# Two side chains of a two-layer trunk on one Trainium2 core: a compact block inverse, a respaced attention, and a shorter weight ring

## The reference

```python
h = x
h = h + gated_deltanet(rms_norm(h), ...)       # layer 0: 32 value heads of 128, 16 key heads
h = h + swiglu_ffn(rms_norm(h), ...)           # hidden width 5632
shared_kv = nsa_shared_kv(h, ...)              # six 512-wide projections, two of them compressed
h = h + nsa_attention(rms_norm(h), shared_kv)  # layer 1: 16 heads, 4 groups of K/V
h = h + swiglu_ffn(rms_norm(h), ...)
return rms_norm(h, final_norm_g)
...
# DeltaNet, per head and chunk: (I + strictly lower(beta k k^T decay)) is inverted, then
v_new = u_c - w_c @ state
o_c = q_c @ state + attn_qk @ v_new
state = state * exp(gl) + k_c^T @ v_new
# attention, per query block: three branches, each a softmax, summed with sigmoid gates
return gb[0] * o_cmp + gb[1] * o_slc + gb[2] * o_win
```

## Time and profile before

| | us |
|---|---|
| three runs, median (lowest to highest) | 2998.84 (2996.97 to 2998.98) |
| the profiled execution, its own time | 3000.31 |
| its span, first to last instruction | 2998.5 |
| TensorE busy in it | 2896.9 |
| VectorE busy | 1837.0 |
| ScalarE busy | 1328.9 |
| mean granted TensorE clock | 0.982 of full |
| read from HBM | 490.02 MB |

### The profile page before, as it was taken

The page is one execution under the profiler, slowest core; times in us unless marked ns, Lnnn a source line. Parts: engine busy times, 40 slices in busy tenths (PEclk is TensorE's granted clock), DMA queues, the critical chain, the costliest instruction groups (busy, mean ns, idle before and its releaser), DMA issues.

```text
span 2998.5 us, 37768 instructions
## 1 busy us (share of the span) xinstructions
PE 2896.9 (97%) x14080; PEld 2433.9 (81%) x14080; DVE 1837.0 (61%) x2200; ACT 1328.9 (44%) x1539; POOL 26.4 (1%) x29
## 2 busy tenths in 40 slices
PE   7999999999999999999999999889989999999997
PEld 6888888888887788888888878778778888888886
DVE  5777877877777645555555554556655555555555
ACT  6445454453543444444444444544435444444443
POOL 0000000000000000000000000000000000000000
PEclk9999999999999999999999999899999999999999
DMA  6333443434433345555555545532325555555553
GB/s 268 136 131 121 165 150 125 161 131 144 159 114 112 140 183 194 185 194 192 188 194 182 195 176 185 197 113 96 129 85 199 194 191 187 191 189 194 188 190 112
DMA packets 69411, 493.11 MB, mean 164 GB/s; under 512 B 7712, under 2 KB 8032, under 8 KB 10592
## 3 DMA queue, kind: packets, MB, share of 16 engines
q1 hardware_dynamic: 68112, 487.95, 45.4%
q10 hardware_dynamic: 1232, 4.23, 0.4%
HBM read 490.02 MB, written 2.13 MB: 164 GB/s over the span
## 4 chain that ended last, share of the span: by engine, by line
issue 57%; PE 40%; DVE 1%; ACT 1%; POOL 0%; DMA 0%; POOLq 0%; ACTq 0%; SPq 0%; DVEq 0%
PE ACC L483 12%; PE ACC L485 12%; PE ACC L484 12%; PE SIDE L491 2%; PE SIDE L772 1%; PE SIDE L751 0%; PE ACC L714 0%; PE SIDE L789 0%; PE ACC L715 0%; ACT WORK L1091 0%; PE SIDE L769 0%; DVE W_LO L1132 0%; DMA RAW<-stream 0%; PE SIDE L779 0%; DVE WORK L1477 0%
## 5 line engine op out<-in xcount | busy, mean ns | idle before, releaser
L1132 DVE TENSOR_TENSOR W_LO<-RAW,W_HI 128x1024 fp32r<-128x1024 f32 x912 | 1100.0, 1222 | 722.1 <-ACT W_HI L831 716.8
L831 ACT ACTIVATE W_HI<-RAW 128x1024 fp32r<-128x1024 f32 x912 | 961.5, 1059 | 1260.9 <-PE ACC L485 1249.6
L483 PE MATMUL ACC<-W_HI,X_HI 128*128 128x512 f32 x2496 | 992.1, 397 | 15.3 <-DVE W_LO L1132 13.3
L485 PE MATMUL ACC<-W_HI,X_LO 128*128 128x512 f32 x2496 | 975.2, 391 | 0.0
L484 PE MATMUL ACC<-W_LO,X_HI 128*128 128x512 f32 x2496 | 973.7, 390 | 0.0
L483 PEld LDWEIGHTS ACC<-W_HI,X_HI 128*128 128x128 f32 x2496 | 471.1, 189 | 108.8 <-issue 14.0
L485 PEld LDWEIGHTS ACC<-W_HI,X_LO 128*128 128x128 f32 x2496 | 469.8, 188 | 100.3
L484 PEld LDWEIGHTS ACC<-W_LO,X_HI 128*128 128x128 f32 x2496 | 471.0, 189 | 92.6 <-issue 0.6
L483 PE MATMUL ACC<-W_HI,A_HI 128*128 128x512 f32 x1088 | 433.6, 398 | 12.9 <-issue 12.9
L485 PE MATMUL ACC<-W_HI,A_LO 128*128 128x512 f32 x1088 | 426.8, 392 | 0.0
L484 PE MATMUL ACC<-W_LO,A_HI 128*128 128x512 f32 x1088 | 426.3, 392 | 0.0
(11 more groups left out here) (216 smaller groups left out, 1584.2 us busy)
## 6 DMA issues: line engine op xcount, KB each, us to landing
RAW<-stream SPq DMA_DIRECT2D x456, 1024.0 KB, 4.8
WORK<-gdn_rows ACTq DMA_DIRECT2D x8, 512.0 KB, 3.6
WORK<-xt SPq DMA_DIRECT2D x4, 512.0 KB, 9.4
H<-x SPq DMA_DIRECT2D x2, 1024.0 KB, 17.8
out<-WORK SPq DMA_DIRECT2D x4, 512.0 KB, 3.9
WORK<-tails SPq DMA_DIRECT2D x2, 512.0 KB, 12.7
WORK<-gfin SPq DMA_DIRECT2D x1, 1024.0 KB, 6.7
K<-consts SPq DMA_DIRECT2D x1, 678.0 KB, 16.2
```

The lines of the kernel that those rows point to most:

```text
L483: nc.tensor.matmul(dst, hi[:, at:at + P], wh, start=first and h % 2 == 0 and q == 0, stop=False)
L485: m = nc.tensor.matmul(dst, lo[:, at:at + P], wh, start=False, stop=last and h % 2 == 1 and q == 1)
L831: nc.scalar.activation(W_HI[:, h % WS, :], raw_piece(h), ACT.Copy).then_inc(hi_ready, 1)
L1132: nc.vector.tensor_tensor(W_LO[:, h % WS, :], raw_piece(h), W_HI[:, h % WS, :].bitcast(f32), SUB).then_inc(lo_ready, 1)
```

## The change

- **The inverse.** The u products are gone. After a t step VectorE transposes T in blocks of 32x32 (`nc.vector.transpose`), and ScalarE copies the result into UQ, UB or UR. At levels 0 to 3 only the four 32x32 diagonal blocks of a unit matter, so y and t get stationaries of 32 columns (the diagonal blocks packed into YB and UQ) and write 32 rows. At levels 4 and 5 both get 64 columns and move 64. ScalarE empties every y, and t of levels 4 and 5; VectorE does t of levels 0 to 3 in four parts. The masks are applied to N beforehand, in a new step `masks`.
- **Room.** VN takes v0 and v1 (before in `cin`), QK1 keeps the later chunk of q and k, NR is used again for the refinement. The first tap of the convolution and k_t move from VectorE to ScalarE.
- **Tables.** SOLVE, LAST, PREP and FIRST steps get new slots.
- **Attention.** `ATT_PIECES` spreads the 64 pieces over the six iterations as 8, 12, 12, 12, 10 and 10, ATT_CHAIN over 12 slots; branches a and b have score tiles and maxima of their own and overlap; the 15 compressed keys' scores share a PSUM buffer with sc0a; groups with an odd number have TR and UR as output operands. The loops over iterations 2 and 3 are unrolled.
- **The stream.** A load is a piece (512 KB), RAW has four places of a piece.

```diff
+        def quad_products(p, lhs, rhs):
+            for u in range(8):
+                m = nc.tensor.matmul(SIDE[p][0:32, u * P:(u + 1) * P], lhs[:, u * 32:(u + 1) * 32],
+                                     rhs[:, u * P:(u + 1) * P], **ONE)
+            m.then_inc(side_full[p], 1)
...
-                unit_products(p, NR, TR)
+                if lv == QUADS:
+                    pe.wait_ge(n_hi, g + 1)
+                if lv < QUADS:
+                    quad_products(p, YB[:, lv * 256:lv * 256 + 256], TR)
+                else:
+                    block_products(p, lv, lambda u: NR[:, u * P + 64 * (lv - QUADS):u * P + 64 * (lv - QUADS) + 64], TR)
             elif kind == "t":
                 gdn_done(pe, f"y{lv}", it)
-                unit_products(p, UR, Y_OF[lv])
-            elif kind == "u":
-                unit_products(p, Y_OF[lv], UR)
+                pe.wait_ge(u_ready, g * STEP_UPS + (lv + 1))
+                if lv < QUADS:
+                    quad_products(p, UQ, YQ)
...
+            elif kind == "u":        # VectorE
+                gdn_done(dve, f"t{lv}", it)
+                t_ = TR[:, :].bitcast(f32)
+                if lv < QUADS:
+                    i = nc.vector.transpose(UF, t_)
...
+            elif kind == "u":        # ScalarE
+                act.wait_ge(u_turned, g * LEVELS + (lv + 1))
+                if lv < QUADS - 1:
+                    for r in range(4):
+                        i = nc.scalar.activation(units(UQ[:, :], 32)[32 * r:32 * r + 32, :, :], quad(UF, r), ACT.Copy)
...
-    0 y0
-    1 t0 u0 conv_v0a
-    2 y1
-    3 t1 u1 conv_v0b
+    0 y0
+    1 t0
+    2 u0 conv_v0a
+    3 y1 conv_v0b
+    4 t1
+    5 u1 conv_v1a y2 strict conv_v1b
+    7 silu_v t2 u2
+    10 y3
+    11 t3 u3
+    13 y4
+    14 t4
+    15 u4 v_t2 y5
+    16 t5 u5 nw
+    18 ru
+    19 v0
+    20 s
+    21 ks
+    22 v1
+    23 o fill
+    24 osum
+    26 oscale
+    30 o_t
...
+ATT_PIECES = [att_run("q", 0),
+              att_run("q", 1) + att_run("q", 2, 0, 4),
+              att_run("q", 2, 4) + att_run("out", 0),
+              att_run("q", 3) + att_run("out", 1, 0, 4),
+              att_run("out", 1, 4) + att_run("out", 2, 0, 6),
+              att_run("out", 2, 6) + att_run("out", 3)]
+ATT_CHAIN = att_table("""
+    0 sc1a sc0a
+    1 mx1a mx0a scc
+    2 sc1b sc0b
+    3 scs mx1b mx0b
+    4 pt1a pt0a
+    6 pva ptc
+    8 pt1b pt0b
+    9 pvc
+    10 pvb
+    11 o_t q_t""")
...
-        RAW = sb("RAW", [P, RAWS, CHUNK])
+        RAW = sb("RAW", [P, RAWS, PIECE])
```

More of the change, by code:

```diff
@@ L143 @@
     14 v0
[L144 to L151, removed]
-    0 y0
-    1 t0 u0 conv_v0a
-    2 y1
-    3 t1 u1 conv_v0b
[L156 to L170, removed]
+    15 s ks
+    16 v1 o
     19 osum oscale
-    21 o_t""")
+    20 o_t""")
 PREP_STEPS = gdn_table(PREP, """
[L174 to L179, removed]
-    15 conv_qk1b
[L181 to L188, removed]
+    1 factors
+    9 dif qk_t
+    10 conv_qk0a
+    11 conv_qk0b conv_qk1a
+    15 conv_qk1b
+    16 silu_qk
+    18 squares decay ss
+    22 qkn beta
+    23 v_t
+    26 qk1 kkqk k_t
+    27 nr init
+    28 masks""")
 FIRST_STEPS = gdn_table(ONCE, """
@@ L192 @@
     13 gates2""") + gdn_table(PREP, """
[L193 to L200, removed]
+    9 qk_t conv_qk0a conv_qk0b
+    10 conv_qk1a
+    11 conv_qk1b
+    15 silu_qk squares
+    17 ss fill qkn factors
+    20 k_t dif v_t
+    21 beta decay kkqk qk1 nr init masks""")
 def gdn_steps(it, hs):
@@ L208, in gdn_steps, with att_run, att_table, att_steps @@
     return [(name, p, which) for h, name, p, which in table if h == hs]
[L211 to L222, removed]
+def att_run(part, g, lo=0, hi=8):
+    return [(part, g, n) for n in range(lo, hi)]
+ATT_PIECES = [att_run("q", 0),
[4 more added lines that the diff above has]
+              att_run("out", 2, 6) + att_run("out", 3)]
+ATT_BASE = [sum(len(p) for p in ATT_PIECES[:it]) for it in range(len(ATT_PIECES))]
+ATT_PAIR = {"gates": 0, "gates_f": 0, "sc1a": 0, "sc0a": 1, "sc1b": 0, "sc0b": 1, "pt1a": 0, "pt0a": 1, "pva": 0,
+            "ptc": 1, "pvc": 1, "pt1b": 0, "pt0b": 1, "pvb": 0, "o_t": 0, "q_t": 1}
+def att_table(text):
+    return [(int(at), name, ATT_PAIR.get(name)) for at, *names in (line.split() for line in text.strip().split("\n"))
+            for name in names]
+ATT_ONCE = att_table("""
+    7 gates
+    8 q_t
+    9 gates_f""")
+ATT_CHAIN = att_table("""
[9 more added lines that the diff above has]
+    11 o_t q_t""")
+def att_steps(it, at):
+    table = {0: ATT_ONCE, KVG + 1: []}.get(it, ATT_CHAIN)
+    return [(name, p, it if name == "q_t" or it == 0 else it - 1) for s, name, p in table
+            if s == at and not (name == "q_t" and it == KVG)]
 class Phase:
@@ L274, in ffn_uses, with att_uses @@
     return uses + ([("x0", "hid_t")] if up else [])
[L277 to L283, removed]
-        uses += [(f"x{p}", n) for n, p, _ in steps_at(ATT_STEPS, hs, which)]
+def att_uses(it):
+    uses, pieces = [], ATT_PIECES[it]
+    for at in range(16):
+        if at < len(pieces):
+            part, g, n = pieces[at]
+            if part == "q" and n == 7:
+                uses.append((f"a{g % 2}", f"q{g}"))
+            if part == "out" and n % 2:
+                uses.append((f"a{n // 2 % 2}", f"out{g}{n // 2}"))
+        uses += [(f"x{p}", f"{name}{g}") for name, p, g in att_steps(it, at) if p is not None]
     return uses
```

486 lines of the change are left out of this document (275 added, 211 removed).

## The result

The changed kernel takes 2952.37 us (median of 4 runs, 2949.19 to 2956.49), the kernel before 2998.06 (4 runs, 2996.97 to 2998.98). The ratio is 0.9849, 95% interval 0.9835 to 0.9864: faster by 1.5%, some 46 us. The forecast was 2893 us with a range of 2868 to 2942, so the sign is right and the time lies 10 us above the range. The profiled execution took 2950.0 us around a span of 2948.2, 50.3 us under the span before.

What follows compares the result with a forecast made beforehand. TensorE, busy 97% of the span, was taken to bound the kernel, with removable waits in attention. Gains of 119.9 us less losses of 14 gave 105.9 off the 2998.84 us median: 2893 us, range 2868 to 2942.

Steps and rivals of the forecast that it cites:

- a piece is wanted about 8 us later: Stream: a load starts when the split four pieces before is done and is wanted about 8 us later; cost 0.
- -1 and +4: Stream at the kernel's start: smaller piece 0 against pieces 4 to 7 queued behind other loads; bounds in us, taken as 0.
- I take 5 left: Attention: 5 us of waits remain after the new order, so 34.4 us gained, bounds 28 and 39.
- followed slot by slot ... some 69 us: Last DeltaNet group, first y to o turn: some 69 us where it was 81.7, with waits at t1, t3, y4.
- each wait can drop the clock: Last group: reason given for bounds -5 and 10 around the 5 us gain taken on top of parts 1 and 2.
- the three terms: DeltaNet TensorE work saved: u off TensorE 42.2 us, 32-column products 22.0, 64x64 products 12.8, over 8 groups.
- rival C: DeltaNet side chains: ScalarE evictions behind a split delay 96 y and t steps by 0.5 us, 48 us: 2941; chance 0.13.
- 2.7 us of piece stand between nearly all: DeltaNet: argument against rival C, that 2.7 us of piece separate nearly all y and t steps.
- the 5.5 us of the earlier trace: First iteration: the 5.5 us wait for qkn is more than half covered by the later slot, 3.5 us less.
- Rival E: Stream: the ring of four pieces starves, W_HI late by 0.3 us in each of 912 pieces, 270 us; chance 0.02.
- Rival D: DeltaNet chains with a full wait at t1 and t3, 1.74 us over 96 steps: 3060 us; chance 0.05.
- wrong if W_LO waits appear in front of pieces: Sign against the forecast: W_LO waits in front of pieces, or transposes over 2.4 us.

Runs made afterwards that it cites:

- run 1: On the kernel before, the stream ring alone changed to four pieces of 512 KB in place of four chunks of 1 MB: 3012.58 us, ratio 1.0046.
- run 2: On the kernel before, a ring of eight pieces of 512 KB, the same 4 MB of room: 2999.65 us, ratio 1.0001.
- run 5: On the changed kernel, a ring of eight pieces instead of four, with VN moved onto YB and WORK trimmed: 2939.22 us, ratio 0.9804.
- run 3: On the changed kernel, attention's exponentials mx1b and mx0b put behind the evictions pt1a and pt0a: 2940.45 us, ratio 0.9808.
- Run 9: On the changed kernel, one more VectorE transpose of 128x1024 ahead of the one at each of levels 0 to 3: 2987.97 us, ratio 0.9965.
- Run 8: On the changed kernel, quad products (levels 0 to 3) taken from stationaries of 128 columns again: 2959.26 us, ratio 0.9873.
- Run 4: On the changed kernel, the last DeltaNet group respaced, two slots from each y to its t and from t5 to nw: 2959.72 us, ratio 0.9867.
- Run 12: Changed kernel with ring of eight, exponentials behind evictions, and first-iteration steps moved (silu_qk, squares to slot 14; kkqk and others to 22): 2924.97 us, ratio 0.9752.

## Why the prediction was wrong, step by step

The forecast took 105.9 us off; the profiled spans differ by 50.3, so 55.6 are missing. They lie as follows; what is not listed moved by 1 us.

| place | forecast | measured | missing |
|---|---|---|---|
| last group, y0 to o_t | -12.7 (69 for 81.7) | +1.6 | 14.3 |
| attention | -34.4 | -21.5 | 12.9 |
| keys, values, compression | 0 | +8.6 | 8.6 |
| five steady groups | -8.6 each | -6.9 each | 8.5 |
| start to the first y0 | -3.5 | +3.5 | 7.0 |
| two groups with few pieces | -5.6 each | -2.8, -4.1 | 4.3 |

The steady groups' forecast is (42.2 + 22.0 + 12.8)/8 = 9.6 less 1.0 for nw, with 3 more taken off for the two with few pieces. By the same terms the last group has 9.6 - 1.0 + 5 = 13.6, about 1 us more than its 69 us give.

**The stream, costed at 0: the step "a piece is wanted about 8 us later" failed.** It is true where a piece keeps TensorE busy for 2.7 us, and I had read it there. In the compression a piece is used for about 1 us, so four pieces are 4 us of cover for a load that takes 3.9 and is issued only when a place comes free. The row that should have warned me was the wait total of the earlier trace rows (4.6 us in 4 waits): 2.2 us of it already lay in this stretch with twice the room. Runs 1, 2 and 5 show it from both sides: 9.4 us lost by the ring alone on the kernel before, 7.8 regained by eight pieces on the changed one, 3 us at the start each time. The ring costs 13 to 14 us in all. The bound "-1 and +4" named only the start.

The Trainium skill ("DMA: Bandwidth & Descriptors", section "Measured (HBM→SBUF, 128 partitions, SWDGE, issued from GpSimd)") asks for 1 MiB and more in a transfer. I had weighed that in the forecast, and it would have warned, but for another reason: eight halves did as well as four wholes here (ratio 1.0001).

**Attention: "I take 5 left" failed.** The groups' work was counted well: a group without waits takes 53.1 us (run 3), which is twelve pieces of 2.73 and the 20.0 us of steps by the earlier trace rows within 0.4. What I left out is the order on ScalarE. I counted slots between a step and its reader on TensorE, not what stands ahead of the eviction in ScalarE's queue. There, exponentials that waited for VectorE held up a finished product. Run 3 shows 9 us of the 12.9. With the ring of eight as well, attention is 268.1 us, 32.6 under before, where 34.4 was forecast; the 2 us between it and run 3 are within the spread of runs. In run 3 TensorE still waits 8.6 us in all where 5 were taken. Of these the 4 us before the last o turn stay in every run; the forecast had 2.6 there. The granted clock, forecast as 1.00 throughout, was 0.94 in the last group of the changed kernel and 0.98 there in run 3. That the branches in flight would fill the gaps was right.

**The last group: "followed slot by slot ... some 69 us" failed, and it is the largest term.** Two parts of it were too small. First the waits: t1, t3 and y4 wait 4.81, 2.22 and 1.29 us, where 3.6, 1.9 and 1.3 were forecast, and t5 and o_t wait 2.67 and 0.79 us, where the forecast had none. That is 5.0 us. Second the clock: the 69 us took every step at its price at full clock, and "each wait can drop the clock" stood only in the bounds. Three stretches of one step and one piece, each right behind a wait, ran at half the clock:

```profile
883.78:889.84 6.06, 6.06 (x21) 4.74 (x22) 5.91 (x13) 1.93 (x4) 0.00 (x0) 0.50 0.54 172
904.01:910.12 6.11, 6.11 (x21) 4.72 (x22) 1.94 (x3) 4.81 (x7) 0.00 (x0) 0.50 0.26 92
917.69:923.83 6.14, 6.14 (x20) 4.98 (x21) 2.96 (x5) 2.11 (x3) 0.00 (x0) 0.50 0.55 173
```

They took 6.06, 6.11 and 6.14 us, where a step and a piece take 3.26, 3.33 and 3.33 at full clock, 8.4 us in all. With the 5.0 us that is 13.4 of the 14.3 missing. Run 3 shows that the clock is paid in full and does not hide in the waits. This group has the same code there and 18.6 us of idle time for 18.0, but behind its wait of 2.85 us at t5 the clock stayed full, and the group took 95.2 us at a mean clock of 0.93 instead of 99.4 at 0.88. The stretch that answers to the third one above, in run 3:

```profile
919.60:922.91 3.31, 3.31 (x21) 2.83 (x22) 2.32 (x4) 1.49 (x2) 0.00 (x0) 1.00 0.50 163
```

So runs with the same code in this group differ by up to 4 us (95.2 to 99.4), and what decides whether the clock falls behind a wait was not found. The waits themselves come from the chain of VectorE update, transpose, ScalarE copies, y eviction and t step, shown above at t1. The change made this chain longer at each level: before, one VectorE operation of 1.22 us evicted y, and u needed no transpose. Run 9 shows that it is on the path: at nearly the same clock (0.89), 5.0 us more on VectorE add 5.2 us of idle time to this group and 4.5 us to its length. Run 8 would show whether TensorE's own steps count there, but its clock was 0.93: it took as long as the changed kernel and 4.0 us longer than run 3, which had that clock too, so it does not decide this. Run 4 shows that moving pieces in this way does not help.

**The steady groups: the price was right, the cover was not.** Quad products cost 0.060 us each, under my 0.067. The 0.056 that the Trainium skill's gap of 134 cycles gives ("TensorE: Matmul & The Clock Gate", section "Back-to-back issue gap"), noted in the forecast, is nearer, and this trace agrees with it within 0.004 us.

One reading behind the price was not like for like: the load record of 96 ns is of a plain fp32 product, and the 192 ns that I set against it of an fp32r one. A plain fp32 load of 128 columns (L491) has a median record of 141 ns, so the record is not halved. VectorE's transposes of 128x1024 take 1.24 us (1.22 forecast), VectorE is busy 87.4 us a group (87), ScalarE 77.6 (78):

```profile
L1439 DVE STREAM_TRANSPOSE WORK<-TR 128x1024 f32<-128x1024 f32 x32 | 39.7, 1242 | 0.6
```

The nw wait of 1.02 us came as forecast. The t3 wait of 1.1 did not: y3's eviction stands on ScalarE behind that of qk_t. It is in the direction of rival C, which has 0.5 us at each of 96 steps; it is one wait of 1.1 us a group. The argument that "2.7 us of piece stand between nearly all" steps hid how little was left of it: run 9 adds 1.24 us at four levels and the group pays 4.5 of 5.0. So DeltaNet's steady group is balanced between TensorE and the chain.

**The first iteration failed in sign.** About 3 us are the ring (runs 1 and 5). The rest is ss and kkqk, which now wait for ScalarE (4.2 and 2.8 us). The likely reason, which no run tested, is that ScalarE took over work of VectorE in just that chain. The forecast had only followed the 5.5 us of the earlier trace rows, which did go. Run 12 halved one of these waits and removed the other, and a wait of 2.7 us for VectorE came in their place: moving the steps alone does not shorten this part by more than the spread of runs.

**Held:** TensorE's work per steady group fell by 9.2 us where the three terms gave 9.6, the feed-forwards kept their time within about 1 us, attention's work was as counted, and the sign was right. Rival E (starving) was right in kind, given 0.02 because I priced it for all 912 pieces; it bites in one stretch. Rival D did not happen. What I had asked to see against me ("wrong if W_LO waits appear in front of pieces") is just what the compression shows.

## What to carry to other kernels

A ring's depth is to be counted in the time of its fastest consumer, not of its usual one: find the stage where a transfer is used up quickest and divide. When work is moved off the busiest engine into a chain of evictions, follow that chain through every engine's own queue, with what stands ahead of it and who next uses the same output, above all where few other tasks fill the gaps; saved TensorE time counts only up to the length of that chain. A wait is to be priced with the clock that can fall behind it: in the last group three stretches at half clock cost 2.8 us each, about as much as the waits ahead of them. And a wait of 1 us in a balanced order can be the cheapest place for it: two plausible one-slot shifts cost 22 and 40 us.

## What the runs showed of the hardware

A stationary of 32 columns nearly halved the price of a step: eight fp32r products of 128 moving columns start 0.060 us apart against 0.110 with 128 columns, though the record of one 32-column load is still 109 ns. A VectorE transpose of 128x1024 fp32 costs what an ordinary operation of that size costs (1.24 us), of 128x512 0.71, while the ScalarE copies that follow it, four of 32x256 at 0.42 us, cost more than the transpose. A step of eight short products and a piece took 3.3 us at a granted clock of 1.00 and 6.1 at 0.50; behind waits of 2.7 and 2.85 us at the same place the clock was 0.50 in one run and 1.00 in another.
